# One subtraction per 512 columns, one accumulating transfer per down piece, and the token sums and LRU rates in parts

## The chip, the cores and the metric

The kernel runs on one core of a Trainium2 chip. The metric is the device time of one execution in microseconds (us); the times are medians of repeated executions on the chip. PE is TensorE, DVE VectorE, ACT ScalarE, POOL GpSimd and SP SyncE.

## What is computed

Two networks of two layers each run one behind the other on 512 tokens of width 1024, all in f32. What matters here are the four feed-forward parts. In the first network (stages mlp0 and mlp1) each has 32 tiles of 128 hidden columns; in the second (layer0 and layer1) 22 tiles of a gate and as many of an up projection, over 528 tokens (16 meta tokens ahead of the 512).

```python
def sq_relu_mlp(h, w_up, w_down):                 # D 1024, FF 4096
    return jnp.square(jax.nn.relu(h @ w_up)) @ w_down

def conv_gated_mlp(n, w_up, conv_w, w_down):      # D 1024, FF 2816
    gate, up = jnp.split(n @ w_up, 2, axis=-1)
    gate = causal_dwconv(gate, conv_w)
    return (jax.nn.silu(gate) * up) @ w_down

def rg_lru(x, w_r, b_r, w_i, b_i, lam):           # in the mixer between mlp0 and mlp1
    ...
    log_a = -LRU_C * r.astype(jnp.float32) * jax.nn.softplus(-lam.astype(jnp.float32))
```

## The kernel before

**Precision.** Every f32 matrix is kept as two fp32r halves, high and low, and each product is three matmuls: high times high, low times high and high times low. So each weight has to be split on the chip before PE can use it.

**The way of a weight.** Weights come as pieces of 128 x 1024 f32 (512 KB). SP loads piece p into one of 4 raw slots (`load_piece`, L722); the load of p + 4 waits until the last part of p has been used by POOL or ACT. ACT rounds a part into `wh` (`w_hi`, L1579). For parts that come as they are ("whole", and the halves "a11", "a12", "a22"), POOL then subtracts: `wl = source - wh` (L811), and counts `w_lo` up. For a "down" part ACT first writes the negated source, rounded, into `wl` (L1578) and then the high half into `wh` (L1579), and a DMA that POOL issues (L805) adds a half of the piece from HBM onto `wl`, so that no engine subtracts it. PE waits for `w_lo` or for the landing of that DMA. `wh` and `wl` are rings of 4 places of 1024 columns, that is 8 halves; `place` is the half at which a part starts, and `w_used` tells when PE is through with one.

**Pairs.** Behind the first tiles of a feed-forward part, which are computed whole (L839; 6 of them, in the layers 3 gates and 3 ups), two tiles at a time are computed as a pair: seven half products in place of eight, in the order a11, s1, a12, s2, s4, s3, a22 (L1074, 12 matmuls each, all on a half of the tokens). s1, s2, s4 and s3 are sums of weight halves, which DVE makes (`weight_sum_of`, L2740, 2742, 2744 and 2746; s3 lies in `square_sum`). They multiply sums of token halves (`token_sum`), which DVE makes once for each feed-forward part (`token_sums`, L2699 to L2713, five groups of four instructions) together with their low halves (`token_sum_low`, L2720), while ACT makes the high ones (`token_sums_high`). ACT keeps three of the products (L1865), and DVE adds them up (`pair_product`, L2754).

**Down pieces.** The hidden tiles go through the down projection one chunk late. In the mlp stages each pair carries two down pieces: a11, s1, a12, s2, s4, s3, down, down, a22, down, down, where each "down" is a half of a piece with 12 matmuls (L1132); PE takes both of a piece one after the other. In the layers each pair carries one down piece (L1136), four of these pairs to a chunk. DVE adds each result to x (L2769).

**Queues.** Each engine works through its own program in order. `Order` lists all parts in the order in which PE uses them, and ACT (`split_before`) and POOL (`for o, ... in enumerate(order.ops)`) follow that list. POOL subtracts a part of 512 columns as two instructions of 256, and sends one DMA for a half of a down piece, when ACT has made its high half and when the DMA four halves before has landed (`LOWS` = 4 semaphores in turn). With 4 raw slots, the load of a pair's second weight piece in the mlp stages, which its sums need, goes out when POOL has subtracted a22 of the pair before.

**Rates.** In mlp0 DVE computes the rates of the next mixer (`lru_rates`, a log1p by a series, some twenty instructions on 128 x 8) at one go before the first pair; ACT makes an exponential for it between the whole tiles and the pairs.

## Time and profile before

| | us |
|---|---|
| median of 3 runs | 2879.78 |
| lowest and highest | 2877.41 and 2883.34 |
| the profiled execution | 2870.28 |
| its span | 2868.5 |
| PE busy | 2745.3 (96%) |
| DVE busy | 1981.5 (69%) |
| POOL busy | 1712.6 (60%) |
| ACT busy | 1317.3 (46%) |
| granted TensorE clock, mean | 0.99 |

The profiled execution is 9.5 us shorter than the median of the runs. The four feed-forward parts with pairs lie at 237 to 600 us (mlp0), 748 to 1100 (mlp1), 1606 to 1990 (layer0) and 2485 to 2868 (layer1); mixers lie between them. PE's busy time is modelled, and an engine's busy time says nothing of what it waited for; that is read from the chain of waits and from timelines.

### The profile page before, as it was taken

What the parts mean: (1) busy time and instruction counts of PE and PEld (TensorE: products, weight loads), DVE (VectorE), ACT (ScalarE), POOL (GpSimd) and SP (SyncE); (2) the same over time, 40 slices, a digit from 0 to 9 for tenths busy, and PEclk for the clock granted to TensorE, in tenths of its full rate; (3) what the DMA queues carried; (4) which work ended last, traced back from release to release, by engine and by line L of the source; (5) the groups of instructions that cost most, each with busy time, mean ns of one, the idle gap of its engine ahead of it and who ended that gap; (6) DMA issues with size and microseconds to landing.
All of it is one profiled execution on the core that took longest, in us unless ns stands there. A gap on an engine that the chain in (4) does not pass through costs nothing.

```text
span 2868.5 us, 48309 instructions
## 1 busy us (share of the span) xinstructions
PE 2745.3 (96%) x18436; PEld 2465.6 (86%) x18436; DVE 1981.5 (69%) x3159; ACT 1317.3 (46%) x2353; POOL 1712.6 (60%) x1908
## 2 busy tenths in 40 slices
PE   9989999999999999999899989999999899989999
PEld 6767888877788988998799989999988799978898
DVE  8957555576746658897654767776798645577775
ACT  4454454555444454443353345455443244345453
POOL 6426677755568775442225489996542125579995
PEclk9999999999999999999999999999999999999999
DMA  5102656632265665323324144545322333334545
GB/s 187 59 26 78 159 140 161 165 118 74 74 159 143 153 156 154 99 74 100 96 82 134 58 114 117 139 126 148 112 82 79 80 98 123 98 89 113 138 127 140
DMA packets 154934, 327.91 MB, mean 114 GB/s; under 512 B 26448, under 2 KB 64720, under 8 KB 154448
## 3 DMA queue, kind: packets, MB, share of 16 engines
q1 hardware_dynamic: 73104, 245.98, 26.5%
q0 software_dynamic: 32256, 56.64, 12.3%
q10 hardware_dynamic: 49344, 22.19, 2.9%
q8 instruction: 148, 2.42, 0.3%
q14 instruction: 82, 0.67, 0.1%
HBM read 306.15 MB, written 18.61 MB: 113 GB/s over the span
## 4 chain that ended last, share of the span: by engine, by line
PE 54%; DVE 17%; POOL 12%; issue 7%; DMA 6%; ACT 3%; ACTq 0%; SPq 0%; DVEq 0%; POOLq 0%
PE acc L839 15%; POOL w_lo L811 11%; PE aux L1074 10%; PE acc L1132 6%; PE acc L1329 5%; DMA w_raw<-in_stream 4%; PE acc L888 3%; PE acc L1136 3%; PE aux L1343 3%; DMA w_lo<-in_stream 2%; DVE index_score L3271 2%; PE acc L1310 2%; PE aux L1310 2%; DVE best L3264 2%; PE acc L872 1%
## 5 line engine op out<-in xcount | busy, mean ns | idle before, releaser
L811 POOL TENSOR_TENSOR w_lo<-w_raw,w_hi 128x256 fp32r<-128x256 f32 x1168 | 1103.4, 1072 | 885.8 <-ACT w_hi L1579 885.6
L1579 ACT ACTIVATE w_hi<-w_raw 128x512 fp32r<-128x512 f32 (+2 forms) x612 | 459.2, 752 | 204.1 <-PE acc L839 142.5
L811 POOL TENSOR_TENSOR w_lo<-weight_sum,w_hi 128x256 fp32r<-128x256 f32 x384 | 389.3, 1062 | 189.6 <-ACT w_hi L1579 188.1
L839 PE MATMUL acc<-n_hi,w_hi 128*128 128x264 f32 (+1 forms) x1368 | 350.6, 319 | 14.0 <-DVE unit_a L3181 6.4
L839 PE MATMUL acc<-n_lo,w_hi 128*128 128x264 f32 (+1 forms) x1368 | 339.3, 311 | 0.0
L839 PE MATMUL acc<-n_hi,w_lo 128*128 128x264 f32 (+1 forms) x1368 | 338.5, 310 | 0.0
L1074 PE MATMUL aux<-token_sum_hi,w_hi 128*128 128x264 f32 (+1 forms) x1024 | 294.1, 287 | 24.9 <-DVE root L2754 13.1
L1074 PE MATMUL aux<-token_sum_lo,w_hi 128*128 128x264 f32 (+1 forms) x1024 | 290.9, 284 | 0.0
L1074 PE MATMUL aux<-token_sum_hi,w_lo 128*128 128x264 f32 (+1 forms) x1024 | 290.6, 284 | 0.0
L1132 PE MATMUL acc<-hidden_hi,w_hi 128*128 128x512 f32 x688 | 274.2, 399 | 9.6 <-DMA w_lo<-in_stream 6.7
L1579 ACT ACTIVATE w_hi<-weight_sum 128x512 fp32r<-128x512 f32 x192 | 120.7, 630 | 341.4 <-DVE weight_sum L2740 292.3
L1132 PE MATMUL acc<-hidden_lo,w_hi 128*128 128x512 f32 x688 | 271.8, 395 | 0.0
L1132 PE MATMUL acc<-hidden_hi,w_lo 128*128 128x512 f32 x688 | 271.7, 395 | 0.0
L839 PEld LDWEIGHTS acc<-n_hi,w_hi 128*128 128x128 f32 x1368 | 224.3, 189 | 45.3 <-issue 21.6
L805 POOL DMA_DIRECT2D w_lo<-in_stream x224 | 215.3, 1144 | 59.5 <-DMA w_lo<-in_stream 38.4
L2754 DVE TENSOR_TENSOR unit_a<-aux,kept_product 128x256 f32<-128x256 f32 (+1 forms) x154 | 65.7, 427 | 253.5 <-PE aux L1074 238.3
L839 PEld LDWEIGHTS acc<-n_lo,w_hi 128*128 128x128 f32 x1368 | 223.1, 189 | 15.9 <-issue 2.6
L839 PEld LDWEIGHTS acc<-n_hi,w_lo 128*128 128x128 f32 x1368 | 222.9, 189 | 13.6
L1074 PEld LDWEIGHTS aux<-token_sum_hi,w_hi 128*128 128x128 f32 x1024 | 194.5, 190 | 34.0 <-issue 23.1
L1074 PE MATMUL aux<-n_hi,w_hi 128*128 128x264 f32 (+1 forms) x768 | 217.7, 283 | 4.9 <-POOL w_lo L811 3.1
L1074 PE MATMUL aux<-n_lo,w_hi 128*128 128x264 f32 (+1 forms) x768 | 216.6, 282 | 0.0
L1074 PE MATMUL aux<-n_hi,w_lo 128*128 128x264 f32 (+1 forms) x768 | 216.6, 282 | 0.0
(529 smaller groups left out, 6729.8 us busy)
## 6 DMA issues: line engine op xcount, KB each, us to landing
w_raw<-in_stream SPq DMA_DIRECT2D x420, 512.0 KB, 3.8
w_lo<-in_stream POOLq DMA_DIRECT2D x192, 256.0 KB, 6.2
unit_blocks<-unit_scratch ACTq DMA_DIRECT2D x26, 256.0 KB, 4.2
w_raw<-in_stream SPq DMA_DIRECT2D x16, 384.0 KB, 4.9
w_lo<-in_stream POOLq DMA_DIRECT2D x32, 192.0 KB, 4.6
unit_scratch<-unit_staged ACTq DMA_DIRECT2D x20, 256.0 KB, 2.8
saved_x<-x SPq DMA_DIRECT2D x2, 2112.0 KB, 10.0
x<-saved_x SPq DMA_DIRECT2D x16, 264.0 KB, 2.8
```

Of the source, the lines that this page charges most:

```text
L805: pool.dma_start(wl[:, slot, at:at + n], stream[p, :, part * n:part * n + n], accum_op=ALU.add)\
L811: i = pool.tensor_tensor(wl[:, slot, at + a:at + z], source[:, a:z], wh[:, slot, at + a:at + z].bitcast(F32), ALU.subtract)
L839: last = pe.matmul(o, w[:, slot_of(p), P * b:P * b + P], r, start=(b == 0 and i == 0), stop=(b == n - 1 and i == 2))
L888: mm = pe.matmul(acc[:, bank_of(p), :], w[:, slot_of(p), P * b:P * b + P], v[b], start=(n == 0 and i == 0), stop=(n == KT - 1 and i == 2))
L1074: mm = pe.matmul(aux[:, bank, 0:width], w[:, slot, at_ + P * b:at_ + P * b + P], v[:, b, :], start=(opens and b == 0 and i == 0), stop=(b ...
L1132: mm = pe.matmul(into, lhs, v[:, e % 2, b, ROW], start=(b == 0 and i == 0), stop=(b == n - 1 and i == 2))
L1136: mm = pe.matmul(banks[:, s, 0:HALF], lhs, v[:, e % 2, b, HALF * s:HALF * s + HALF], start=(b == 0 and i == 0), stop=(b == n - 1 and i == 2))
L1310: mm = pe.matmul(banks[:, 2 * g + s, 0:HALF], w[:, slot_of(p), P * b:P * b + P], v[:, b, HALF * s:HALF * s + HALF], start=(b == 4 * g and ...
L1329: mm = pe.matmul(acc[:, s, 0:HALF], w[:, slot_of(p), P * b:P * b + P], v[:, b, HALF * s:HALF * s + HALF], start=(b == 0 and i == 0), stop= ...
L1343: return pe.matmul(out, lhs, rhs, start=start, stop=stop)
L1579: act.activation(wh[:, slot, at_:at_ + n], weights_of(o), ACT.Copy).then_inc(w_hi, 1)
L2754: dve.tensor_tensor(into, aux[:, bank, 0:width], kept_product[:, kept, 0:width], ALU.add)\
```

## The change

**POOL** subtracts up to 512 columns in one instruction where it took 256: 840 instructions for 1680. A down piece is sent by one DMA for both halves where its place in the ring allows it (79 of 128 x 1024, 14 of 128 x 2 x 384) and by two where it would wrap around (38 DMAs): 131 in place of 224. It waits for the high halves of both parts and for the piece four before. The first piece of a pair is sent ahead of the subtraction of s3. PE waits for the whole piece before its first half.

**Token sums** are made one at a time between the whole tiles, by DVE and by ACT, and the weight sums of the first pair are put among later tiles. In the layers a whole tile is cut into its gate and its up part for that.

**Rates**: the same instructions, at the pairs 2, 4, 6, 8 and 10 of mlp0; ACT's exponential stands at s4 of the fourth pair (u is 3).

```diff
-        self.low, self.sent, low, sent = [], [], 0, 0
-        for kind, _, _ in self.ops:
-            low, sent = low + (kind != "down"), sent + (kind == "down")
+        self.low, self.sent, low, sent = [], {}, 0, [0] * LOWS
+        for o, (kind, _, part) in enumerate(self.ops):
+            low += kind != "down"
             self.low.append(low)
-            self.sent.append(sent)
+            if kind == "down" and part == 0:
+                n = len(self.sent) // 2 % LOWS
+                before, sent[n] = sent[n], sent[n] + 16 * len(self.transfers(o))
+                self.sent[o] = self.sent[o + 1] = (n, before, sent[n])
         self.sums, sums = {}, 0
         for feed in self.feeds.values():
             for q in feed["pieces"]:
                 sums += len(SUMS)
                 self.sums[q] = sums
+
+    def transfers(self, o):
+
+        return [(o, 2)] if self.place[o] + 1 < 2 * W_SLOTS else [(o, 1), (o + 1, 1)]
...
-    def low_landed(d):
-
-        return low_of[d % LOWS], 16 * (d // LOWS + 1)
+    def low_landed(o):
+
+        return low_of[order.sent[o][0]], order.sent[o][2]
...
+        def send(first):
+
+            n, before, _ = order.sent[first]
+            if before:
+                pool.wait_ge(low_of[n], before)
+            for o, halves in order.transfers(first):
+                _, p, part = order.ops[o]
+                slot, at = order.half(o)
+                w = width_of(o)
+                pool.wait_ge(w_hi, o + halves)
+                into = wl[:, slot, at:at + w]
+                if halves == 2:
+                    into = wl[:, :, :].rearrange("p s c -> p (s c)").rearrange("p (h c) -> p h c", c=KT // 2 * P)[
+                        :, order.place[o]:order.place[o] + 2, 0:w]
+                    source = stream[p, :, 0:2 * w].rearrange("p (h c) -> p h c", h=2)
+                else:
+                    source = stream[p, :, part * w:part * w + w]
+                pool.dma_start(into, source, accum_op=ALU.add).then_inc(low_of[n], 16)
+
+        def subtract(o):
             slot, at = order.half(o)
             n = width_of(o)
             source = weights_of(o)
-            if kind == "down":
-                d = order.sent[o] - 1
-                if d >= LOWS:
-                    pool.wait_ge(*low_landed(d - LOWS))
-                pool.wait_ge(w_hi, o + 1)
-                pool.dma_start(wl[:, slot, at:at + n], stream[p, :, part * n:part * n + n], accum_op=ALU.add)\
-                    .then_inc(low_landed(d)[0], 16)
-                continue
             pool.wait_ge(w_hi, o + 1)
-            for a in range(0, n, 2 * P):
-                z = min(a + 2 * P, n)
+            for a in range(0, n, 4 * P):
+                z = min(a + 4 * P, n)
                 i = pool.tensor_tensor(wl[:, slot, at + a:at + z], source[:, a:z],
                                        wh[:, slot, at + a:at + z].bitcast(F32), ALU.subtract)
             i.then_inc(w_lo, 1)
+
+        for o, (kind, _, part) in enumerate(order.ops):
+            ahead = o + 1 < len(order.ops) and order.ops[o + 1][0] == "down"
+            if kind == "s3" and ahead:
+                send(o + 1)
+            if kind == "down":
+                if part == 0 and order.ops[o - 1][0] != "s3":
+                    send(o)
+            else:
+                subtract(o)
...
-                    pe.wait_ge(*low_landed(order.sent[o] - 1))
+                    pe.wait_ge(*low_landed(o))
...
-                if i == 1:
-                    token_sums_high(stage)
                 hidden_high(i)
-            if layer == 0:
-                act.wait_ge(cent_ready, 5)
-                act.activation(c8[:, 1, :], c8[:, 0, :], ACT.Exp, scale=-1.0)\
-                    .then_inc(ln_root, c.made(ln_root))
+                for n in ((0,), (1,), (2, 3))[i] if i < 3 else ():
+                    token_sum_high(stage, n)
...
+                if layer == 0 and kind == "s4" and u == 3:
+                    act.wait_ge(cent_ready, 5)
+                    act.activation(c8[:, 1, :], c8[:, 0, :], ACT.Exp, scale=-1.0)\
+                        .then_inc(ln_root, c.made(ln_root))
...
+        def lru_rates(u):
+
+            if u == 2:
+                rates_in()
+            elif u == 4:
+                dve.wait_ge(ln_root, 2)
+                log1p_begin(c8[:, 1, :], RATE_PARTS, c8[:, 0, :])
+            elif u == 6:
+                log1p_terms(RATE_PARTS, c8[:, 0, :], (15, 13, 11, 9))
+            elif u == 8:
+                log1p_terms(RATE_PARTS, c8[:, 0, :], (7, 5, 3))
+            elif u == 10:
+                log1p_end(RATE_PARTS, c8[:, 0, :])
+                rates_out()
...
-        def token_sums(stage, gains):
+        def token_sum(stage, gains, n):
 
             first, second = halves_of(stage)
             width = first.stop - first.start
             low, high = range(KT // 2), range(KT // 2, KT)
-            t1, t2, t3, t4 = ([tf[:, n, k, 0:width] for k in low] for n in range(4))
+            t = [tf[:, n, k, 0:width] for k in low]
 
             def ended(k, i):
                 ready = t_sum if k == KT // 2 - 1 else dve_seq
                 i.then_inc(ready, c.made(ready))
                 return c.mine()
 
-            difference = [step(dve.tensor_tensor(t1[k], x[:, k, second], x[:, k, first], ALU.subtract)) for k in low]
-            made = []
+            if n == 0:
+                difference = [step(dve.tensor_tensor(t[k], x[:, k, second], x[:, k, first], ALU.subtract)) for k in low]
+                for k in low:
+                    dve.wait_ge(*difference[k])
+                    at["sum"] = ended(k, dve.tensor_scalar(t[k], t[k], gains(k), None, ALU.mult))
+                return
+            if n < 3:
+                dve.wait_ge(*at["sum"])
+            tiles, part = ((high, second), (low, first), (high, first))[n - 1]
             for k in low:
-                dve.wait_ge(*difference[k])
-                made.append(ended(k, dve.tensor_scalar(t1[k], t1[k], gains(k), None, ALU.mult)))
-            made2 = []
-            for k in low:
-                dve.wait_ge(*made[k])
-                made2.append(ended(k, dve.scalar_tensor_tensor(t2[k], x[:, high[k], second], gains(high[k]), t1[k],
-                                                               ALU.mult, ALU.subtract)))
-            for k in low:
-                dve.wait_ge(*made2[k])
-                ended(k, dve.scalar_tensor_tensor(t3[k], x[:, k, first], gains(k), t2[k], ALU.mult, ALU.subtract))
-            for k in low:
-                ended(k, dve.scalar_tensor_tensor(t4[k], x[:, high[k], first], gains(high[k]), t2[k],
-                                                  ALU.mult, ALU.subtract))
+                i = dve.scalar_tensor_tensor(t[k], x[:, tiles[k], part], gains(tiles[k]), tf[:, min(n - 1, 1), k, 0:width],
+                                             ALU.mult, ALU.subtract)
+                at["sum"] = ended(k, i)
...
             whole(0)
-            token_sums(stage, gains)
+            token_sum(stage, gains, 0)
             whole(1)
+            token_sum(stage, gains, 1)
             token_sum_low(stage, 0)
             whole(2)
+            token_sum(stage, gains, 2)
+            token_sum(stage, gains, 3)
+            whole(3)
             token_sum_low(stage, 1)
             weight_sum_of(stage, 0, "s1")
             weight_sum_of(stage, 0, "s2")
-            whole(3)
+            whole(4)
             token_sum_low(stage, 2)
             weight_sum_of(stage, 0, "s4")
+            whole(5)
             token_sum_low(stage, 3)
-            whole(4)
             weight_sum_of(stage, 0, "s3")
-            whole(5)
             low()
             if layer:
                 two_norms_ahead()
-            else:
-                lru_rates()
...
+                    if layer == 0:
+                        lru_rates(u)
...
-            def whole(i):
-                b = i % 2
+            def whole_gate(i):
                 a = full()
-                dve.tensor_tensor(wide(ub[:, b, :]), a, wscale, ALU.mult).then_inc(taken, c.made(taken))
+                dve.tensor_tensor(wide(ub[:, i % 2, :]), a, wscale, ALU.mult).then_inc(taken, c.made(taken))
                 mine = c.mine()
                 if waiting:
                     low()
                 convolve(i, mine)
-                conv = c.mine()
+                return c.mine()
+
+            def whole_up(i, conv):
                 a = full()
                 dve.wait_ge(*conv)
-                dve.tensor_tensor(wide(ub[:, b, :]), a, wscale, ALU.mult).then_inc(taken, c.made(taken))
-                gated(i, ub[:, b, :], c.mine())
-
-            whole(0)
-            token_sums(stage, gains)
-            whole(1)
+                dve.tensor_tensor(wide(ub[:, i % 2, :]), a, wscale, ALU.mult).then_inc(taken, c.made(taken))
+                gated(i, ub[:, i % 2, :], c.mine())
+
+            conv = whole_gate(0)
+            token_sum(stage, gains, 0)
+            whole_up(0, conv)
+            token_sum(stage, gains, 1)
+            conv = whole_gate(1)
+            token_sum(stage, gains, 2)
+            token_sum(stage, gains, 3)
+            whole_up(1, conv)
             token_sum_low(stage, 0)
             weight_sum_of(stage, 0, "s1")
+            conv = whole_gate(2)
             token_sum_low(stage, 1)
             weight_sum_of(stage, 0, "s2")
-            whole(2)
+            whole_up(2, conv)
+            weight_sum_of(stage, 0, "s4")
             token_sum_low(stage, 2)
-            weight_sum_of(stage, 0, "s4")
+            weight_sum_of(stage, 0, "s3")
             token_sum_low(stage, 3)
-            weight_sum_of(stage, 0, "s3")
```

The rest of the diff cuts `log1p` into `log1p_begin`, `log1p_terms` and `log1p_end`, and `lru_rates` into `rates_in` and `rates_out`, and does in ACT's layer program what is shown of its mlp program.

POOL in mlp0, before; one step of two down pieces. `square_sum` is s3, the next `w_raw` is a22, and behind the second transfer come a11, s1, a12, s2 and s4 of the next pair:

```order
L811 TENSOR_TENSOR w_lo<-square_sum,w_hi 128x256 x2
L805 DMA w_lo<-in_stream 128x512 x2
L811 TENSOR_TENSOR w_lo<-w_raw,w_hi 128x256 x2
L805 DMA w_lo<-in_stream 128x512 x2
L811 TENSOR_TENSOR w_lo<-w_raw,w_hi 128x256 x2
L811 TENSOR_TENSOR w_lo<-weight_sum,w_hi 128x256 x2
L811 TENSOR_TENSOR w_lo<-w_raw,w_hi 128x256 x2
L811 TENSOR_TENSOR w_lo<-weight_sum,w_hi 128x256 x4
```

The same place on POOL, changed:

```order
L820 DMA w_lo<-in_stream 128x1024
L829 TENSOR_TENSOR w_lo<-square_sum,w_hi 128x512
L829 TENSOR_TENSOR w_lo<-w_raw,w_hi 128x512
L820 DMA w_lo<-in_stream 128x1024
L829 TENSOR_TENSOR w_lo<-w_raw,w_hi 128x512
L829 TENSOR_TENSOR w_lo<-weight_sum,w_hi 128x512
L829 TENSOR_TENSOR w_lo<-w_raw,w_hi 128x512
L829 TENSOR_TENSOR w_lo<-weight_sum,w_hi 128x512 x2
```

The first transfer of the step has moved ahead of s3, and each row of two instructions is one of twice the width.

DVE at the first whole tiles of mlp0, before. L2814, L2804 and L2809 are a tile; L2699 to L2713 the token sums:

```order
L2814 SCALAR_TENSOR_TENSOR unit_a<-acc,norm_scale 128x512
L2809 TENSOR_TENSOR unit_b<-unit_a 128x512
L2699 TENSOR_TENSOR token_sum<-x 128x256 x4
L2703 TENSOR_SCALAR token_sum<-token_sum,vec_61 128x256 x4
L2707 SCALAR_TENSOR_TENSOR token_sum<-x,vec_61,token_sum 128x256 x4
L2711 SCALAR_TENSOR_TENSOR token_sum<-x,vec_61,token_sum 128x256 x4
L2713 SCALAR_TENSOR_TENSOR token_sum<-x,vec_61,token_sum 128x256 x4
L2814 SCALAR_TENSOR_TENSOR unit_a<-acc,norm_scale 128x512
L2804 TENSOR_TENSOR hidden_lo<-unit_b,hidden_hi 128x512
L2809 TENSOR_TENSOR unit_b<-unit_a 128x512
```

The same place on DVE, changed:

```order
L2870 SCALAR_TENSOR_TENSOR unit_a<-acc,norm_scale 128x512
L2865 TENSOR_TENSOR unit_b<-unit_a 128x512
L2757 TENSOR_TENSOR token_sum<-x 128x256 x4
L2760 TENSOR_SCALAR token_sum<-token_sum,vec_61 128x256 x4
L2870 SCALAR_TENSOR_TENSOR unit_a<-acc,norm_scale 128x512
L2860 TENSOR_TENSOR hidden_lo<-unit_b,hidden_hi 128x512
L2865 TENSOR_TENSOR unit_b<-unit_a 128x512
L2766 SCALAR_TENSOR_TENSOR token_sum<-x,vec_61,token_sum 128x256 x4
L2776 TENSOR_TENSOR token_sum_lo<-token_sum,token_sum_hi 128x4x256
L2870 SCALAR_TENSOR_TENSOR unit_a<-acc,norm_scale 128x512
```

Eight of the twenty token-sum instructions are left ahead of the second tile; the other twelve stand behind it and behind the third.

## Rows read from the trace of the kernel before

**Rows 1.** The page, busy time of each engine.
```profile
PE 2745.3 (96%) x18436; PEld 2465.6 (86%) x18436; DVE 1981.5 (69%) x3159; ACT 1317.3 (46%) x2353; POOL 1712.6 (60%) x1908
```

**Rows 2.** Windows: stretch, length, busy of PE to POOL, clock, DMA share, GB/s.
```profile
324.00:559.00 235.00, 233.45 (x1454) 208.30 (x1453) 142.69 (x199) 112.59 (x223) 180.52 (x197) 1.00 0.60 146
833.00:1066.00 233.00, 231.98 (x1457) 207.87 (x1455) 143.77 (x201) 113.23 (x223) 180.16 (x197) 1.00 0.61 148
1606.00:1715.00 109.00, 93.81 (x722) 91.56 (x721) 81.30 (x108) 43.86 (x81) 71.05 (x77) 0.95 0.34 86
1715.00:1958.00 243.00, 238.02 (x1935) 235.63 (x1933) 186.17 (x257) 126.81 (x247) 225.21 (x240) 1.00 0.49 125
```

**Rows 3.** Chain that ended last, mlp0: start us, us, what.
```profile
394.62 8.26 POOL w_lo L811 x8
...
416.67 8.26 POOL w_lo L811 x8
...
487.59 8.44 PE aux L1074 x72
...
508.59 8.44 PE aux L1074 x72
```

**Rows 4.** Line L811, whole span: count, duration ns min/median/max, starts.
```profile
L811 POOL TENSOR_TENSOR w_lo<-w_raw,w_hi x1168: 720/1078/3825, 8.3 to 2831.5; 128x256 fp32r<-128x256 f32 x195
```

**Rows 5.** Timeline of DVE in a step of mlp0: start us, us, operation.
```profile
523.26 0.68 DVE L2744 TENSOR_TENSOR weight_sum<-w_raw,weight_sum 128x512 f32<-128x512 f32 x1
523.86 1.23 DVE L2804 TENSOR_TENSOR hidden_lo<-unit_b,hidden_hi 128x512 fp32r<-128x512 f32 x1
...
525.90 1.23 DVE L2746 TENSOR_TENSOR square_sum<-w_raw 128x512 f32<-128x512 f32 x1
527.05 1.22 DVE L2809 TENSOR_TENSOR unit_b<-unit_a 128x512 f32<-128x512 f32 x1
```

**Rows 6.** Timeline of ACT in the same step.
```profile
528.30 0.63 ACT L1876 ACTIVATE hidden_hi<-unit_b 128x512 fp32r<-128x512 f32 x1 [3.69 <-DVE unit_b L2809]
...
530.92 0.62 ACT L1579 ACTIVATE w_hi<-w_raw 128x512 fp32r<-128x512 f32 x1
```

**Rows 7.** Timeline of POOL in the same step.
```profile
530.23 1.90 POOL L811 TENSOR_TENSOR w_lo<-square_sum,w_hi 128x256 fp32r<-128x256 f32 x2
532.07 1.77 POOL L805 DMA_DIRECT2D w_lo<-in_stream  x2
533.22 2.08 POOL L811 TENSOR_TENSOR w_lo<-w_raw,w_hi 128x256 fp32r<-128x256 f32 x2
```

**Rows 8.** Landing of loads at 514.7; of sends at 532.1, 534.6, 1921.2.
```profile
DMA to landing us min/median/max: 6.1/7.2/8.3
...
DMA to landing us min/median/max: 4.1/4.9/5.7
...
DMA to landing us min/median/max: 9.9/10.2/10.5
...
DMA to landing us min/median/max: 4.2/5.3/6.4
```

**Rows 9.** Chain that ended last, layer0: start us, us, what.
```profile
1898.67 8.77 PE aux L1074 x72
...
1921.16 4.21 DMA w_lo<-in_stream
...
1925.42 6.11 PE acc L1136 x48
1931.53 8.76 PE aux L1074 x72
```

**Rows 10.** Waits of PE at 236 to 324: us, times, longest.
```profile
PE acc L839 <- POOL w_lo L811: 3.0, 1, 3.0
```

**Rows 11.** Waits of PE at 1606 to 1715.
```profile
PE aux L1074 <- DVE root L2754: 5.7, 2, 5.4
PE acc L839 <- DVE unit_a L3181: 3.2, 1, 3.2
```

**Rows 12.** Timeline of DVE at the first tiles of layer0.
```profile
1616.69 3.11 DVE L2699 TENSOR_TENSOR token_sum<-x 128x264 f32<-128x264 f32 x4
```

More of the change, by code:

```diff
@@ L794, in _ @@
     def _(pool):
-        for o, (kind, p, part) in enumerate(order.ops):
+        def send(first):
[16 more added lines that the diff above has]
+        def subtract(o):
             slot, at = order.half(o)
@@ L1847, in mixer1, with token_sum_high @@
             last_jobs(SEQ, STAGES[-1] != "mix1", lambda k: vec("mlp_norm", 8 + k))
-        def token_sums_high(stage):
-            parts = halves_of(stage)
-            width = parts[0].stop - parts[0].start
-            for n in range(4):
-                act.wait_ge(t_sum, c.next(t_sum))
-                act.activation(th[:, n, :, 0:width], tf[:, n, :, 0:width], ACT.Copy).then_inc(n_hi, c.made(n_hi))
+        def token_sum_high(stage, n):
+            width = halves_of(stage)[0].stop - halves_of(stage)[0].start
+            act.wait_ge(t_sum, c.next(t_sum))
+            act.activation(th[:, n, :, 0:width], tf[:, n, :, 0:width], ACT.Copy).then_inc(n_hi, c.made(n_hi))
         def keep_product(o, u, width):
@@ L2103, in layer @@
                 gate_silu(i)
-                if i == 1:
-                    token_sums_high(stage)
+                if i == 0:
+                    token_sum_high(stage, 0)
                 split_before(used(at["piece"] + 1))
@@ L2108, in layer @@
                 hidden_high(i)
+                if i == 0:
+                    token_sum_high(stage, 1)
+                elif i == 1:
+                    token_sum_high(stage, 2)
+                    token_sum_high(stage, 3)
             for o in feed["ops"][:-KT]:
@@ L2572, in log1p, with log1p_terms, log1p_end, rates_in @@
             dve.wait_ge(*step(dve.tensor_scalar(sum_, s2, 1.0 / 17.0, None, ALU.mult)))
-            for n in (15, 13, 11, 9, 7, 5, 3):
-                dve.wait_ge(*step(dve.scalar_tensor_tensor(sum_, sum_, 1.0 / n, s2, ALU.add, ALU.mult)))
-            dve.wait_ge(*step(dve.scalar_tensor_tensor(sum_, sum_, 1.0, s, ALU.add, ALU.mult)))
-            dve.wait_ge(*step(dve.tensor_scalar(sum_, sum_, 2.0, None, ALU.mult)))
-        def lru_rates():
+        def log1p_terms(tmp, sum_, terms):
+            for n in terms:
+                dve.wait_ge(*step(dve.scalar_tensor_tensor(sum_, sum_, 1.0 / n, tmp[2], ALU.add, ALU.mult)))
+        def log1p_end(tmp, sum_):
+            dve.wait_ge(*step(dve.scalar_tensor_tensor(sum_, sum_, 1.0, tmp[1], ALU.add, ALU.mult)))
+            dve.wait_ge(*step(dve.tensor_scalar(sum_, sum_, 2.0, None, ALU.mult)))
+        def log1p(e, tmp, sum_):
+            log1p_begin(e, tmp, sum_)
+            log1p_terms(tmp, sum_, (15, 13, 11, 9, 7, 5, 3))
+            log1p_end(tmp, sum_)
+        RATE_PARTS = (c8[:, 3, :], c8[:, 4, :], c8[:, 5, :])
+        def rates_in():
             lam = v1[:, V1["c_lambda"][0]:V1["c_lambda"][1]]
```

7 lines of the change are left out of this document (4 added, 3 removed).

## The prediction

> **What bounds the kernel now.** I read the busy times of the page first. PE is busy 2745 of 2868.5 us and no other engine comes near [rows 1], so an edit can only take away idle time of PE, or add to it. The windows say where that idle time is: 1.6 us in the 235 us of mlp0's steady part, 1.0 us of 233 in mlp1, 5 us of 243 in layer0, but 15 us of 109 in the beginning of layer0, where the granted clock is 0.95 too [rows 2]. So the steady parts have next to nothing to give, and the beginnings have.
>
> The chain of waits comes next, since busy shares don't tell how near the feeders are. In mlp0 the chain runs over POOL from 394.62 to 416.67, 22.0 us a step, and further on over PE, 21.0 from 487.59 to 508.59 [rows 3]. 21.0 is what PE needs when nothing holds it, and the eleven steps of mlp0 take 235, that is 21.4 each; those of mlp1 take 233, 21.2 each [rows 2]. So a second loop runs beside PE at nearly its pace: the one that makes the weights ready.
>
> The timelines show this loop. A load goes out at 514.7 when POOL is done with a22, and the first lands 6.1 later, at 520.8 [rows 8]. DVE then makes four sums, with tile work between, until `squared` ends at 527.05 + 1.22 = 528.27 [rows 5]. ACT makes hidden_hi, the high half of s3 and both halves of the down piece, until 530.92 + 0.62 = 531.54 [rows 6]. POOL ends s3 at 532.1, sends two DMAs, and does a22 from 533.22 to 535.30 [rows 7]. There the next load goes out: 20.6 us in this step, with no PE in it. It has 0.4 us to spare against 21.0.
>
> **The wider subtraction.** An instruction of 256 columns takes 0.72 us at least and 1.08 in the median [rows 4]. DVE's operations with two operands in SBUF take 0.68, and 1.23 when they meet one of POOL's [rows 5]: DVE sits out the rest of POOL's instruction, 0.55 us, and POOL sits out DVE's, which is how 0.72 becomes 1.08. With 512 columns the alone time can't be under one of 256, 0.72, and not over two, 1.44. POOL's cost grows with the columns, so I take 1.3, near the upper end: a fixed share of 0.1 or so is saved. The Trainium skill (GPSIMD Engine Reference, 3.1 Elementwise — side-by-side cycle accounting) has 4497 ns for 2048 columns, from which one estimates, at a fixed cost of 0.1 to 0.2, 1.2 for 512; by that the term of this part would be about 2.0 and not 2.4 in the next paragraph, and the mlp steps 22.3.
>
> In the loop, DVE passes POOL's instructions one by one between the landing and `squared`, about four times (three of them show in [rows 5] as a 1.2 where it would be 0.68). Each pass now waits up to 1.3 - 0.72 = 0.6 longer: 4 x 0.6 = +2.4. The bound below is nothing, if POOL and DVE happen to miss each other. The Trainium skill (SBUF — State Buffer, Who interferes with whom) says that the one who issues first holds the shared ports for its whole instruction; at 256 columns the trace agrees, and at 512 no row here shows it.
>
> What comes back: POOL's own waits are halved, at 0.5 for each pair of instructions. In the last leg, from ACT's end at 531.54 on, the send is issued at once and not behind s3; then s3 (1.3, of which 0.6 to 1.1 is left) and a22 (1.3 for 2.08 before) follow. a22 ended 535.30 - 531.54 = 3.8 after ACT; now one DMA (about 0.9, half of the 1.77), 1.3 and 1.3 make 3.5 or less. So 0.3 to 0.8 of the 2.4 comes back, and the loop grows by 1.6 to 2.1; I take 1.8. From 20.6 to 22.0 it goes to 22.4 to 23.8, over PE's 21.0 everywhere. As the loop is stretched, POOL and DVE meet less, so I take the lower part, 22.7. For 22 steps: 22 x 22.7 = 499, for 468 before: **+31**. Bounds: 21.0 (-6) and 23.6 (+51).
>
> **One transfer for a piece.** Two sends of 256 KB landed 4.1 and 5.7 us after their issue, and in the layer 4.2 and 6.4 [rows 8]. PE now waits for all of it. A single DMA moves what the two moved, so it should land where the second did: 5.9 to 7.0 after its issue (bound below 4.1, above 6.4 + 1.1 for the issue that is not spread). In mlp, the first piece has slack (sent at 531.5, needed by PE at 508.59 + 21.0 + 8.44 = 538.0 [rows 3]), the second hasn't: its halves took 9.9 and 10.5 from 534.6 on [rows 8], so 545 to 546 for the last, and PE wants it some 6 to 7 us behind the first (half of 21.0 - 8.44 = 12.6, or a little more), at 544.3 to 545. It is late by about 1 us, but inside a step that is longer by more than that, so I add nothing.
>
> In the layers it is on the path. PE ends s4 at 1898.67 + 8.77 = 1907.44; POOL sends the next piece at 1921.16, 13.7 later, it lands 4.2 later, and PE goes on at 1925.42: 18.0. From there to the end of the s4 after is 6.11 + 8.76 = 14.9 [rows 9]. These are two steps: 32.9, or 16.4 each; the mean of the fifteen steps is 243 / 15 = 16.2 [rows 2]. The send now goes before s3, 1.4 earlier, and the subtractions ahead of it save about as much as DVE's passes lose, so it stands at 12.5; with 5.9 to 7.0 that is 18.4 to 19.5. Step: (18.4 + 14.9) / 2 = 16.7 to 17.2, that is +0.2 to +0.8 on 16.4. Not all steps hang on it; I take +0.3 for each of the 30 steps of both layers: **+9**. Bounds -3 and +24. The Trainium skill (DMA: Bandwidth & Descriptors, Anatomy of one DMA — SWDGE (gpsimd) path) gives a DMA of this kind 2.0 us and its bytes at 436 GB/s, which is 3.2 for 512 KB; by that this term is -3, see the rivals.
>
> **Token sums in parts.** In layer0 twenty instructions start at 1616.69 [rows 12] in one go, and PE waits 3.2 for the tile behind them [rows 11]. That wait goes: only eight stand there now. With POOL's fewer and the sends' earlier issue the first down piece comes a few us earlier, and the 5.4 at the first step with s1 late [rows 11] is worked off earlier by some 2. I take 6 + 2 for each layer, -16. In the mlp stages the wait for the feed is 3.0 [rows 10], behind POOL; I take half of it each, -3. **-19** together; bounds -30 (all 15 us that PE idles in a beginning, twice) and -5 (the two waits of 3.2 alone, and something lost by longer locks).
>
> **Rates in parts**: the same instructions of DVE, on 8 columns and so far shorter than the 0.68 of 512 [rows 5], put where DVE has idle time (142.69 busy of 235 [rows 2]). Nothing, if DVE has room; they come into the loop of five steps, and 0.5 to 1 us each at worst lies inside the range. The mixers have no pairs and no down DMAs, only subtractions off the path: nothing.
>
> **Sum.** On the profiled execution of 2870.3: +31 + 9 - 19 = +21, or 2891. The median lies 9.5 higher, so +21 on 2879.8: **2901 us**.
>
> **Rivals.**
> (a) PE's pace holds, and only the beginnings gain. A 512-column instruction costs DVE no more than 0.1 us in the mean, because the order of the two engines locks into place, or POOL's halved waits make up for it. Then mlp goes to 21.0 (-6), the layers to PE's pace (-3), the beginnings -19: -28, **2852**. For it: the loop has 0.4 to spare where it takes 20.6, and POOL, busy for 180 of 235 us [rows 2], gets less to do. Against: the loop goes through DVE's passes, not through POOL's total. It decides for faster if the loop grows by under 0.9 or so (22 steps x 0.9 = 19).
> (b) The losses are nearer their bounds: 1.44 for an instruction, mlp steps 23.4 (+47), layer steps at +0.7 (+21), the beginnings only -5: +63, **2943**.
> (c) They cancel: the loop grows by 1.2 where it binds, mlp +15 to +18 and layers +4, against -19: **2881**.
> (d) A single transfer beats two. By its own setup it would land at 3.2 to 4.2 and not 5.9 to 7.0. The layers then lose nothing (-3), mlp still +31, beginnings -19: +9, **2889**. The rows speak against it, as the two halves landed 1.6 and 2.2 apart with issues 0.6 apart, so bytes count.
>
> **How the numbers follow.** Forecast 0.38, (a) 0.28, (b) 0.15, (c) 0.12, (d) 0.07. Within 0.2%, 5.8 us, is about what a measurement of this kernel can't tell from no change. Slower is the forecast, (b) and (d): 0.60; faster 0.28; same 0.12. The forecast alone runs from 2888 to 2925. To leave out no more than 2 in 10, the range takes (a) down to 2848 and (b) up to 2945. As both signs count, both are given.
>
> **What would show it.** In the profile after: L829 at 1.25 to 1.4 us at least (under 1.1 and (a) gains); DVE's two-operand operations in a step at 1.8 where they were 1.23; the first down matmuls of mlp steps 22.4 to 23.4 apart, not 21.0, with the chain over POOL, DVE and the load of `w_raw`; transfers of 512 KB landing 5.9 to 7 after issue in the layers, with PE waiting for them at most steps; the wait of PE for L3181's successor gone. I'm wrong if the mlp steps stay at 21.0 to 21.4: then the lock's length isn't passed on to the loop.

## The result, and the profile after

| | median us | runs | against before |
|---|---|---|---|
| before | 2878.6 | 4 | |
| changed | 2941.5 | 4 (2938.7 to 2949.3) | 1.0239 (1.0222 to 1.0257) |

The change costs 63 us by the two medians (their ratio is 1.0219) and 69 by the ratio on record, where 21 were forecast (2901 for 2880). The sign and the range held, the size didn't. The profiled executions have spans of 2868.5 and 2947.0, 78.5 apart; the one of before was among its shortest, the one of after the longest of its kind, so stretches below add up to 78 and not to 63.

The page of the changed kernel: the busy line [rows 1], the chain by engine, and POOL's largest group.

```profile
PE 2771.9 (94%) x18436; PEld 2482.4 (84%) x18436; DVE 2149.0 (73%) x3159; ACT 1327.6 (45%) x2353; POOL 1333.6 (45%) x975
...
PE 50%; DVE 25%; issue 10%; DMA 8%; ACT 6%; POOL 1%; ACTq 0%; DVEq 0%; SPq 0%; POOLq 0%
...
L829 POOL TENSOR_TENSOR w_lo<-w_raw,w_hi 128x512 fp32r<-128x512 f32 x584 | 873.5, 1534 | 1018.0 <-ACT w_hi L1607 1017.9
```

POOL is busy for 1334 us in place of 1713, and it has all but left the chain. DVE is busy for 167 us more with the same 3159 instructions: it does nothing more, it waits inside them. POOL's time was saved where nobody needed it, and DVE paid.

The windows of the same stretches [rows 2] (length, then busy us of PE, PEld, DVE, ACT, POOL, clock, DMA share, GB/s):

```profile
324.00:559.00 235.00, 230.84 (x1426) 205.28 (x1425) 144.77 (x217) 115.55 (x218) 123.93 (x102) 1.00 0.57 145
833.00:1066.00 233.00, 229.49 (x1435) 205.15 (x1434) 136.11 (x191) 113.59 (x215) 126.23 (x102) 1.00 0.60 147
1606.00:1715.00 109.00, 98.71 (x762) 96.34 (x762) 90.05 (x101) 46.09 (x78) 56.77 (x39) 0.97 0.29 79
1715.00:1958.00 243.00, 222.94 (x1777) 217.36 (x1775) 217.56 (x237) 112.35 (x220) 156.60 (x111) 1.00 0.44 117
```

In the mlp stages PE idles 4 us where it idled 1 or 2, and DVE is no busier (144.8 for 142.7 in mlp0). In the layer PE idles 20 for 5, and DVE is busy 217.6 of 243 where it was 186.2. That is where the time went.

PE runs the same 18436 matmuls in the same order in all kernels here. So the n-th can be set against the n-th, and the growth of its delay over a stretch is what that stretch costs. In us, on one profiled execution each; kernels are told apart below. Executions of one kernel differ by several us (the one before by 2864 to 2884 over all its runs), so a difference of 2 or 3 says nothing:

| stretch (times of before) | changed | wide only | transfers only | sums only | changed at 256 | s3 first | mixed | whole at 256 |
|---|---|---|---|---|---|---|---|---|
| mixers and ends | +19.0 | +15.0 | +3.8 | +1.4 | +1.3 | +14.1 | +1.8 | -3.2 |
| beginnings of the four feeds | -2.8 | +3.8 | -2.5 | -4.1 | -20.2 | -10.3 | -21.5 | -8.2 |
| mlp steady and last downs | +11.0 | +7.3 | +5.6 | -0.9 | +4.6 | +9.5 | -2.1 | +7.1 |
| layers steady | +50.6 | +15.3 | +10.2 | +0.8 | +14.0 | +15.4 | +3.1 | +47.9 |

### The profile page after: what moved, and what is told of

Its sections match the earlier page's. It is cut to its first block, busy times and chain, and to the rows that moved or that the text cites. A ratio compares the mean times of both kernels' runs of the same rounds, so it can differ in the third digit from the quotient of the medians.

```text
span 2947.0 us, 47272 instructions
## 1 busy us (share of the span) xinstructions
PE 2771.9 (94%) x18436; PEld 2482.4 (84%) x18436; DVE 2149.0 (73%) x3159; ACT 1327.6 (45%) x2353; POOL 1333.6 (45%) x975
## 4 chain that ended last, share of the span: by engine, by line
PE 50%; DVE 25%; issue 10%; DMA 8%; ACT 6%; POOL 1%; ACTq 0%; DVEq 0%; SPq 0%; POOLq 0%
PE acc L867 12%; PE acc L1160 10%; DMA w_lo<-in_stream 7%; PE aux L1102 6%; PE acc L1357 4%; PE acc L916 3%; PE aux L1371 3%; ACT w_hi L1607 2%; PE acc L1164 2%; PE acc L1338 2%; PE aux L1338 2%; ACT w_lo L1606 2%; DVE index_score L3337 1%; DVE best L3330 1%; DVE weight_sum L2798 1%
## 5 line engine op out<-in xcount | busy, mean ns | idle before, releaser
L829 POOL TENSOR_TENSOR w_lo<-w_raw,w_hi 128x512 fp32r<-128x512 f32 x584 | 873.5, 1534 | 1018.0 <-ACT w_hi L1607 1017.9
L829 POOL TENSOR_TENSOR w_lo<-weight_sum,w_hi 128x512 fp32r<-128x512 f32 x192 | 291.5, 1527 | 294.3 <-ACT w_hi L1607 294.1
L1102 PE MATMUL aux<-token_sum_hi,w_hi 128*128 128x264 f32 (+1 forms) x1024 | 295.6, 289 | 36.1 <-ACT kept_product L1891 16.6
L2825 DVE TENSOR_TENSOR x<-x,acc 128x512 f32<-128x512 f32 (+1 forms) x224 | 153.1, 685 | 137.8 <-PE acc L1160 126.5
L820 POOL DMA_DIRECT2D w_lo<-in_stream x131 | 122.2, 959 | 278.1 <-ACT w_hi L1607 276.5
```

The source lines that it names most:

```text
L820: pool.dma_start(into, source, accum_op=ALU.add).then_inc(low_of[n], 16)
L829: i = pool.tensor_tensor(wl[:, slot, at + a:at + z], source[:, a:z], wh[:, slot, at + a:at + z].bitcast(F32), ALU.subtract)
L1102: mm = pe.matmul(aux[:, bank, 0:width], w[:, slot, at_ + P * b:at_ + P * b + P], v[:, b, :], start=(opens and b == 0 and i == 0), stop=(b ...
L2825: dve.tensor_tensor(xm, xm, a, ALU.add).then_inc(taken, c.made(taken))
```

## What happens in a layer step

DVE and POOL in one step of layer0, changed kernel: start us, us, operation, and in brackets the idle time before it.

```profile
1887.15 0.87 POOL L820 DMA_DIRECT2D w_lo<-in_stream  x1 [2.14 <-ACT w_hi L1607]
1887.76 1.59 POOL L829 TENSOR_TENSOR w_lo<-square_sum,w_hi 128x512 fp32r<-128x512 f32 x1
1889.03 2.78 POOL L829 TENSOR_TENSOR w_lo<-w_raw,w_hi 128x512 fp32r<-128x512 f32 x2
```

```profile
1888.23 4.16 DVE L3213 TENSOR_TENSOR hidden_lo<-unit_b,hidden_hi 128x528 fp32r<-128x528 f32 x1 [0.83 <-ACT hidden_hi L2124]
1892.32 0.42 DVE L2810 TENSOR_TENSOR unit_a<-aux,kept_product 128x264 f32<-128x264 f32 x1
```

DVE's subtraction for hidden_lo starts at 1888.23, while s3 is under way on POOL, and ends at 1892.39. POOL's three subtractions s3, a22 and a11 end at 1889.03 + 2.78 = 1891.81. So DVE didn't sit out the one that it met, but all three, and ran its own 0.6 behind them. The same operation in the kernel before:

```profile
1921.12 0.70 DVE L3154 TENSOR_TENSOR hidden_lo<-unit_b,hidden_hi 128x528 fp32r<-128x528 f32 x1
```

It took 0.70. POOL issued its two transfers from 1921.16 on, between s3 and a22, and in that gap DVE got in. The change sends ahead of s3, and the gap is gone.

Not every series of POOL holds DVE so. Some 6 us earlier in the same step s2 and s4 follow each other without idle time too, behind a wait for ACT and not behind a transfer:

```profile
1881.67 3.33 POOL L829 TENSOR_TENSOR w_lo<-weight_sum,w_hi 128x512 fp32r<-128x512 f32 x2 [1.29 <-ACT w_hi L1607]
```

```profile
1882.68 1.16 DVE L2802 TENSOR_TENSOR square_sum<-w_raw 128x512 f32<-128x512 f32 x1
```

DVE's operation ends at 1883.84, and POOL's pair at 1885.00: DVE got in between the two. Over the whole trace of the changed kernel a DVE operation with two inputs in SBUF began during one subtraction, outlasted it and met a next one that followed without idle time, 235 times. In the 34 where POOL's series stood right behind a transfer that it had issued, DVE sat out the second subtraction too; in the other 201 it never did. So what the early send made is a series of three that starts right behind a DMA issue.

The chain of waits of the changed kernel, layer0, one turn:

```profile
1870.61 0.95 DVE hidden_lo L3213
1871.56 2.99 issue
1874.55 0.43 DVE unit_a L2810
...
1888.23 0.96 DVE hidden_lo L3213
1889.20 3.12 issue
1892.32 0.43 DVE unit_a L2810
```

From the product at 1874.55 to the same one a turn later, at 1892.32, it is 17.77 us, and in between the chain holds DVE and ACT but no PE. The 3.0 and 3.1 of "issue" behind hidden_lo are the wait on POOL.

## The experiments

Two theories. **Width**: DVE loses because each subtraction of POOL holds it for 1.26 and not 0.72. **Run**: it loses where POOL works without a break, and the send order took the break away.

### Only the wide subtraction

```diff
-            for a in range(0, n, 2 * P):
-                z = min(a + 2 * P, n)
+            for a in range(0, n, 4 * P):
+                z = min(a + 4 * P, n)
```

> The kernel before, with POOL subtracting 512 columns in one instruction and nothing else changed. Two theories. Width: DVE waits for the longer instruction, so this part alone brings most of the loss, 2920 to 2940 us, layer steps 17.3 to 17.9 us and hidden_lo (128x528) over 3 us in the layers. Run: in the layers DVE's hidden_lo only loses where it meets several subtractions of POOL without a break; here the two sends still stand between s3 and a22, so hidden_lo stays at 0.7 to 1.5 us, the layer steps at 16.1 to 16.8, and the time is 2875 to 2900 us.

2919.0 us, ratio 1.0155 (1.0141 to 1.0169): +44. The time is 1 us short of Width's range, hidden_lo (3.07 in the median) just inside it, and the layer steps (16.7 us) are Run's. All calls of it in the steady part:

```profile
L3154 DVE TENSOR_TENSOR hidden_lo<-unit_b,hidden_hi x15: 1826/3067/3489, 1745.4 to 1979.4; 128x528 fp32r<-128x528 f32 x15
```

and one of them, with POOL beside it:

```profile
1912.57 3.09 DVE L3154 TENSOR_TENSOR hidden_lo<-unit_b,hidden_hi 128x528 fp32r<-128x528 f32 x1 [0.83 <-ACT hidden_hi L2098]
```

```profile
1909.30 1.50 POOL L811 TENSOR_TENSOR w_lo<-square_sum,w_hi 128x512 fp32r<-128x512 f32 x1
1910.74 1.77 POOL L805 DMA_DIRECT2D w_lo<-in_stream  x2
1912.05 3.04 POOL L811 TENSOR_TENSOR w_lo<-w_raw,w_hi 128x512 fp32r<-128x512 f32 x2
```

The other operations of DVE had grown by their meetings, so that hidden_lo came 0.5 us after the gap and waited for a22 and a11, two of them, which here stand right behind the transfers. The gap exists, but it has to be hit.

### Only the transfers

The hunks of `Order`, `low_landed`, `send` and PE's wait on the kernel before, with 256 columns.

```diff
+        def send(first):
...
             for a in range(0, n, 2 * P):
                 z = min(a + 2 * P, n)
...
+            if kind == "s3" and ahead:
+                send(o + 1)
```

> The kernel before, with one transfer per down piece sent ahead of s3, and 256 columns for an instruction of POOL. Width: no loss, 2870 to 2890 us, hidden_lo under 1.5 us. Run: s3, a22 and a11 are now six subtractions back to back, as long as three of 512; hidden_lo of the layers takes 3.5 to 4.2 us as in the changed kernel, layer steps are 17.2 to 17.8, and the time is 2915 to 2935 us.

2884.3, ratio 1.0036 (1.0023 to 1.0048): +9. Run was nearly right on hidden_lo, of which it expected 3.5 to 4.2:

```profile
L3182 DVE TENSOR_TENSOR hidden_lo<-unit_b,hidden_hi x15: 707/4390/5010, 1745.9 to 1976.5; 128x528 fp32r<-128x528 f32 x15
```

It takes 4.39 in the median at 256 columns too, behind six instructions. So the wait goes with the length of the run, not with the width. But the time didn't follow: it lies in Width's range, and the layer steps are 16.6, not 17.2 to 17.8. A wait of 3.7 us more had most of its room in the loop.

### Only the token sums and the rates

The hunks of `token_sum`, `lru_rates` and their callers on the kernel before; POOL and PE as they were.

```diff
-            whole(0)
-            token_sums(stage, gains)
-            whole(1)
+            conv = whole_gate(0)
+            token_sum(stage, gains, 0)
+            whole_up(0, conv)
...
```

> The kernel before, with the token sums one by one and the rates in parts, and nothing else. Both theories: a gain in the beginnings of the four feed-forward parts. As I forecast it, 19 us; as the changed kernel's trace shows it (its beginnings gained 3 to 4 us each in mlp0 and layer0 and nothing in the others), 3 to 10 us: 2868 to 2876 us.

2866.3, ratio 0.9972 (0.9961 to 0.9984): -9 in the same comparison, 2 us under the range of 2868 to 2876. This part is a gain, of half the size that I gave it. What PE waits for at 1606 to 1715 now [rows 11]:

```profile
PE aux L1074 <- DVE root L2782: 6.0, 3, 5.2
PE aux L1074 <- POOL w_lo L811: 4.1, 4, 1.2
PE acc L1136 <- DMA w_lo<-in_stream: 2.8, 2, 1.6
PE acc L839 <- DVE unit_a L3221: 0.7, 1, 0.7
```

The 3.2 behind the token sums is 0.7, as forecast; the 5.4 at the step with two down pieces is still there, as 5.2.

### Width and order crossed

The changed kernel at either width, with the first transfer ahead of s3 or behind it:

```diff
             if kind == "s3" and ahead:
+                subtract(o)
                 send(o + 1)
-            if kind == "down":
+            elif kind == "down":
```

> The changed kernel, but with s3 subtracted before the first transfer of its pair is sent, as before the change. Run: the send is then a break between s3 and a22 in which hidden_lo gets in, at 0.7 to 2.5 us in place of 4.1, and the layer steps fall from 17.8 to 16.4 to 17.0: 2895 to 2920 us. Width: the send order is no cause, hidden_lo stays at 3 us or more and the time within 10 us of 2941.

> The changed kernel with 256 columns for an instruction of POOL again. If the loss needs both the wide instruction and the early send (both lie on one loop through DVE and ACT that had some 2 us of slack a layer step), then what is left is the sum of the two parts alone, +9 for the transfers and -9 for the token sums: 2870 to 2882 us, layer steps 16.2 to 16.7, though hidden_lo still takes over 4 us. If the early send alone were the cause of the layers' loss, the steps stay at 17.2 or more and the time over 2900.

> The changed kernel with 256 columns and with s3 subtracted ahead of the send: one transfer per down piece and the token sums are what is left of the change. If the early send costs at 256 columns too, this is 3 to 8 us shorter than the changed kernel at 256 columns, 2865 to 2874 us; if what costs is that PE waits for a whole piece, it is the same or longer, 2874 to 2885.

The four medians come from three comparisons, in which the kernel before took 2874 to 2879:

| median us (ratio) | sent ahead of s3 | sent behind s3 |
|---|---|---|
| 512 columns | 2941.5 (1.0239) | 2906.0 (1.0106) |
| 256 columns | 2869.6 (0.9983) | 2887.4 (1.0049) |

The widths are 72 us apart in the first column and 19 in the second; the early send costs 35 at 512 columns and gains 18 at 256. So the two parts can't be priced apart. With s3 first at 512 columns the time is Run's (2895 to 2920). The changed kernel at 256 columns is at the lower edge of what was expected (2870 to 2882), where that range took the transfers alone (+9) and the sums alone (-9) for terms to be added. They are not quite: it is 4 us under the kernel before, and its beginnings gained 20 where the two parts alone gained 2.5 and 4.1. hidden_lo in the layers, changed kernel at 256:

```profile
L3213 DVE TENSOR_TENSOR hidden_lo<-unit_b,hidden_hi x14: 709/4325/4973, 1748.2 to 1965.5; 128x528 fp32r<-128x528 f32 x14
```

and at 512 with s3 first, where it passes two and not three (Run had 2.5 at most):

```profile
L3214 DVE TENSOR_TENSOR hidden_lo<-unit_b,hidden_hi x16: 709/2762/3286, 1738.7 to 1987.7; 128x528 fp32r<-128x528 f32 x16
```

The steps of layer0 (from one first down matmul to the next, in the mean) say why width and order don't add up. Before, they are 16.2, which is nearly PE's own pace. Width alone gives 16.7, the transfers alone 16.6, both 17.8. But 16.7 and 16.6 are two different limits. What PE waited for at 1745 to 1960 us (us, times, longest), first with width alone, then with the transfers alone:

```profile
PE aux L1074 <- ACT kept_product L1865: 5.5, 11, 1.2
```

```profile
PE acc L1164 <- DMA w_lo<-in_stream: 5.7, 11, 1.0
```

With width alone the loop through DVE and ACT sets the step. There every further wait of DVE counts: the early send takes hidden_lo from 3.07 to 4.16, 1.1 more, and the step from 16.7 to 17.8. At 256 columns the transfer sets it, and the send order has no part in that: with s3 first the steps are 16.6 as well. The loop through DVE and ACT mostly has room at this width, though hidden_lo takes 4.3. How much room isn't seen, since PE waits for the transfers before it would wait for that loop.

The miss was with 256 columns and s3 first: I allowed 2865 to 2874, or 2874 to 2885 if waiting for whole pieces costs, and it is 2887. Against the early send at this width the beginnings of the feeds lose most (-6.4 in place of -20.2): there the piece comes late. At 1606 to 1718 us PE waits for transfers for 5.1 us, 3.3 at the longest, where it is 2.5 and 0.8 with the early send, which makes up for PE's waiting for both halves.

### A break put back in

POOL waits ahead of a22 of a layer pair until DVE has made hidden_lo; the work and the sends stay.

```diff
+        hold, tiles = {}, 0
...
+                    if kind == "a22" and u:
+                        hold[o] = tiles + feed["whole"] // 2 + u
...
+            if o in hold:
+                pool.wait_ge(h_ready, hold[o])
```

> The changed kernel (512 columns, early send), but in the layers POOL waits ahead of its subtraction a22 until DVE has made hidden_lo. Nothing else is moved and no work is taken away. If DVE's wait behind an unbroken run of POOL is the cause, hidden_lo takes 0.7 to 2.0 us in place of 4.1, layer steps fall from 17.8 to 16.4 to 17.0, and the time is 2895 to 2918 us. If the added wait only moves the delay to POOL, the steps stay at 17.5 to 18.2 and the time over 2930.

2925.0, ratio 1.0178 (1.0161 to 1.0196): 17 us less than the changed kernel, and 7 more than Run allowed. The timeline of DVE, layer0:

```profile
1916.38 1.68 DVE L3224 TENSOR_TENSOR hidden_lo<-unit_b,hidden_hi 128x528 fp32r<-128x528 f32 x1 [0.30 <-ACT hidden_hi L2135]
1918.58 0.43 DVE L2821 TENSOR_TENSOR unit_a<-aux,kept_product 128x264 f32<-128x264 f32 x1 [0.51 <-PE aux L1113]
1919.05 0.96 DVE L3294 TENSOR_TENSOR unit_a<-unit_a,norm_scale 128x528 f32<-128x528 f32 x1
1919.92 1.75 DVE L2807 TENSOR_TENSOR weight_sum<-w_raw 128x512 f32<-128x512 f32 x1
```

hidden_lo falls from 4.16 to 1.68, as Run has it. Of the 2.5 us, 1.1 come back at once: the sum s1, 0.69 in the changed kernel, now meets the a11 that was put off, and takes 1.75. The steps are 17.2, between 17.8 and the 16.4 to 17.0 expected. So the run is a cause, shown by breaking it, and part of the wait only moves. The same run shows what kind of series it takes. POOL beside it:

```profile
1915.90 1.59 POOL L829 TENSOR_TENSOR w_lo<-square_sum,w_hi 128x512 fp32r<-128x512 f32 x1
1918.14 2.98 POOL L829 TENSOR_TENSOR w_lo<-w_raw,w_hi 128x512 fp32r<-128x512 f32 x2 [0.66 <-DVE hidden_lo L3224]
```

a22 and a11 still follow each other without idle time, now behind a wait. DVE's operation at 1919.05 began during a22 and ended at 1920.01, in the middle of a11's time: it got in between the two that it had to sit out in the changed kernel.

> The same added wait with 256 columns. hidden_lo falls from over 4 us to under 1.5; the layer steps have little to give at this width (16.1 to 16.3), so 3 to 8 us shorter than the changed kernel at 256 columns, 2864 to 2876 us.

2868.8, ratio 0.9974 (0.9964 to 0.9985), at 256 columns, against 2869.6 without the wait. That is no difference that can be told. The time is in the range, but the 3 to 8 us expected of the wait aren't there: hidden_lo falls to 1.4 us, and at this width its wait had room.

### The wide subtraction outside the pairs

```diff
-            for a in range(0, n, 4 * P):
-                z = min(a + 4 * P, n)
+            step = 2 * P if order.ops[o][0] == "whole" else 4 * P
+            for a in range(0, n, step):
+                z = min(a + step, n)
```

> The changed kernel, with 256 columns for the whole pieces (the mixers and the first tiles of the feed-forward parts) and 512 for the parts of the pairs. If the wide instruction costs in the mixers too, by DVE's short chains there, this is 12 to 22 us shorter than the changed kernel, 2919 to 2930 us, with the stretches of the mixers back at their lengths before. If the delay of the mixers is carried over from the pairs, it is 2936 to 2944.

2915.2, ratio 1.0146 (1.0124 to 1.0168): 26 us less than the changed kernel, 4 more than the most that I expected. The mixers are back at their lengths (-3 for +19 in the table). They have no pairs, and I had priced them at nothing. A group of DVE there, at 1100 to 1600 us; before, then changed:

```profile
L2960 DVE SCALAR_TENSOR_TENSOR delta_q<-unit_a,vec,delta_q 128x528 f32<-128x528 f32 x12 | 11.7, 974 | 0.4
```

```profile
L3019 DVE SCALAR_TENSOR_TENSOR delta_q<-unit_a,vec,delta_q 128x528 f32<-128x528 f32 x12 | 15.2, 1268 | 0.7 <-ACT delta_q L1989 0.4
```

0.3 us for each of these operations, and DVE has no room there: in the kernel before it was busy for 49 of 50 us at 1240 to 1290.

```profile
1240.00:1290.00 50.00, 48.37 (x382) 44.24 (x382) 49.13 (x115) 17.30 (x22) 19.34 (x26) 1.00 0.20 64
```

### The best of it

256 columns, token sums in parts, and the early single transfer only where it gained: behind the first four pairs of a layer and the first of an mlp stage.

```diff
+    def early(self, o):
+        ...
+                return u < (4 if stage.startswith("layer") else 1)
...
-            if kind == "s3" and ahead:
+            if kind == "s3" and ahead and order.early(o + 1):
```

> Token sums in parts and 256 columns; one early transfer per down piece only behind the first four pairs of a layer and the first pair of an mlp stage, two transfers behind s3, as before the change, everywhere else. The beginnings gained 20 us with the early transfer (256 columns) and 4 without it, the steady parts lost 18 with it and nothing without. If both hold apart, this keeps both gains: 2852 to 2862 us, shorter than the kernel before and all others here. If the early transfers gained only by what they cost later (a phase that is moved), it is at 2864 to 2872.

2853.6, ratio 0.9932 (0.9914 to 0.9951): the shortest of all, 24 us under the kernel before by the medians of the same comparison, 20 by the ratio, and as expected if both gains hold apart. The beginnings keep their 21 us and the steady parts stay where they were. The gain of the beginnings is real, and not one that has to be paid back.

## Why the prediction was off

The terms of the sum were +31 for mlp, +9 for the layers, -19 for the beginnings and 0 for the mixers; on the profiled executions they are +11, +51, -3 and +19. The layers lie outside their own bounds (-3 and +24), the beginnings outside theirs (-30 and -5). That the time still fell into the range, 4 us from its end, is luck: mlp was 20 too high, and made up for part of what the layers, the mixers and the beginnings were too low by (42, 19 and 16).

- **What bounds the kernel**: right, PE with a feeding loop close behind it. But the only such loop that I measured was that of the mlp stages. In the layers I followed the transfer, and not the loop through DVE and ACT that came to set the step.
- **The alone time of the wide instruction**, 1.3: right, it is 1.26 at least.
- **Mlp, +31**: it was +11 on the profiled execution, the last down pieces and the stages' ends with it. The steps are 21.7 and 21.6 us where I had 22.7; before they were 21.4 and 21.2. The step that failed is "about four passes, each 0.6 longer". A pass isn't fixed. In the step at 504 to 508 us of the changed kernel, three operations that I had counted at 1.8 are at their alone time:

```profile
504.39 0.68 DVE L2860 TENSOR_TENSOR hidden_lo<-unit_b,hidden_hi 128x512 fp32r<-128x512 f32 x1
...
505.33 1.46 DVE L2920 SCALAR_TENSOR_TENSOR unit_a<-unit_a,norm_scale 128x256 f32<-128x256 f32 x1
506.71 0.68 DVE L2802 TENSOR_TENSOR square_sum<-w_raw 128x512 f32<-128x512 f32 x1
507.31 0.68 DVE L2865 TENSOR_TENSOR unit_b<-unit_a 128x512 f32<-128x512 f32 x1
```

  [rows 5] had 1.23, 1.23 and 1.22 for them. Half as many instructions of POOL are met about half as often. Of DVE's 88 operations of this kind (128x512, two inputs in SBUF) in the window, 48 waited before and 22 in the changed kernel, and the mean wait went from 0.5 to 0.6 us, not to twice; DVE's busy time in the window grew by 2 us in 235. What the mlp stages did lose is the term that I set to nothing, the second piece of which PE now needs both halves: from the first matmul of the first piece to that of the second PE takes 10 us more, summed over the steps of both stages, and for the rest of the steps 2 to 3 less. The chain there, from the send of a second piece to its 24 matmuls:

```profile
494.12 0.50 issue
494.62 10.31 DMA w_lo<-in_stream
504.93 0.04 issue
504.97 5.87 PE acc L1160 x24
```

- **One transfer in the layers, +9**: the layers lost 51. The transfers alone lost 10 there, so as a price for them the term was about right; width alone lost 15, and the two together 25 more than that. The landing isn't the reason; it was shorter than the 5.9 to 7.0 that I took. From issue to landing at 1740 to 2000 us in the changed kernel:

```profile
DMA to landing us min/median/max: 3.8/5.5/9.8
```

  What failed is "the subtractions ahead of it save about as much as DVE's passes lose", with the early send as a plain gain of 1.4. I looked at what the moved send is ahead of, and not at what had used the place it left. By it and the width hidden_lo waits 3.5 us in each step, on a loop that the width had brought past PE's pace.
- **The beginnings, -19**: -3, and -4 to -9 for the token sums by themselves. The wait of 3.2 went as forecast. The 5.4 stays with the token sums alone (5.2) and falls to 1.6 with the transfers alone, where PE waits 3.7 for ACT in its place and the 3.2 stays. Both parts together, at 256 columns, leave 0.8 and 0.7 of the two waits, and the beginnings gain 20. At 512 the gain is gone again, and PE waits 4.3 in layer0's for ACT's kept product; that the longer waits of DVE are behind it is likely and not shown.
- **The rates, 0**: they were run only together with the token sums, and together these gained. What they cost or gain by themselves stays open.
- **The mixers, 0**: +19. "Off the path" was said of POOL, which is true; DVE is on it, and pays for POOL.
- **The rivals**: (b) gave 2943, and 2941 was measured, but not by its steps: it had +47 in mlp and +21 in the layers. (d), one transfer that lands at 3.2 to 4.2, is refuted: in the layers the single transfers landed 3.8 to 9.8 after their issue, 5.5 in the median. From the formula of the Trainium skill (DMA: Bandwidth & Descriptors, Anatomy of one DMA — SWDGE (gpsimd) path) one estimates 3.2 for 512 KB; the trace decides. On the lock the Trainium skill (SBUF — State Buffer, Who interferes with whom) speaks of the one instruction that was issued first; here DVE waited for two more that POOL started after it.

## What to carry to other kernels

Before merging instructions of an engine that shares something with another, ask who waits for it and not how busy it is: POOL gave back 379 us of its own time, DVE spent 167 more, and the kernel got 63 longer. When an instruction is moved, look at its old place too, and at what now stands right behind it: a DMA issue between two subtractions was the gap through which the other engine got in, and a series right behind one is what it can't get into. And where one part of a change has brought a loop past the pace of the engine that sets the time, the next wait on this loop counts in full: prices don't add up, so try the parts crossed.

## What was new of the hardware

A DVE operation with two inputs in SBUF that meets a series of POOL subtractions which starts right behind a DMA issue of POOL waits for the whole series: 4.16 us for three of 512 columns, 4.4 for six of 256, 3.09 for two of 512, and 1.68 when POOL was held after the first. In other series of 512 columns DVE got in after one subtraction, though POOL had no idle time between two there either. Counted over the traces, DVE sat out the next one too in 34 of 34 meetings behind a DMA issue and in 0 of 201 others (the changed kernel), in 30 of 30 and 0 of 269 (wide only), in 30 of 30 and 0 of 249 (s3 first), and in 0 of 234 where the added wait had broken up the series. At 256 columns a DMA issue ahead is not enough: 33 of 66 and 0 of 504 (transfers only), 11 of 22 and 0 of 563 (before).

Why DVE doesn't get in behind a DMA issue is not shown. In the changed kernel POOL's next subtraction starts 0.3 to 0.5 us before the one ahead of it ends where the series stands behind a DMA issue (1889.03 against 1887.76 + 1.59 = 1889.35), and 0.03 to 0.06 before in the others, so it may be in line before DVE is let in. At 256 columns 30 of the 33 meetings behind a DMA issue in which DVE got in had the short overlap (transfers only), which speaks for it. No run here changes the overlap and nothing else.
